# Grouped-query attention in a two-block kernel: value projections placed behind the query projections, their weights' low parts made by GpSimd

## The reference, cut to what matters

```
def attention_module(hx, hc, wq, wk, wv, wo, q_g, k_g, cos, sin, need_ctx):
    qx = apply_rope(rmsnorm((hx @ wq).reshape(B, S, 16, 64), q_g), cos, sin)
    kx = apply_rope(rmsnorm((hx @ wk).reshape(B, S, 4, 64), k_g), cos, sin)
    vx = (hx @ wv).reshape(B, S, 4, 64)
    kc = rmsnorm((hc @ wk).reshape(B, L, 4, 64), k_g)
    vc = (hc @ wv).reshape(B, L, 4, 64)
    k_all = concatenate([kx, kc]); v_all = concatenate([vx, vc])
    # softmax(q k_all / 8) v_all, four query heads on each key head, then @ wo
```

## Time and profile before

| what | value |
|---|---|
| median of 3 runs | 3340.39 us (3338.66 to 3344.8) |
| the profiled execution, first to last instruction | 3345.0 us |
| PE busy | 3225.9 us (96%) |
| DVE busy | 1487.9 us (44%) |
| ACT busy | 1193.4 us (36%) |
| POOL busy | 763.8 us (23%) |
| granted clock of PE, mean | 0.988 of full speed |

### The profile page before, as it was taken

One profiled execution on the slowest core, in us unless ns is written; L12 is line 12 of the kernel. 1 busy time (PEld: TensorE's weight loads), 2 busy tenths in 40 slices (PEclk: granted clock), 3 DMA queues, 4 the chain that ended last, 5 costly groups with the idle time before them and its releaser, 6 DMA issues.

```text
span 3345.0 us, 38977 instructions
## 1 busy us (share of the span) xinstructions
PE 3225.9 (96%) x15760; PEld 2474.1 (74%) x15760; DVE 1487.9 (44%) x2166; ACT 1193.4 (36%) x1764; POOL 763.8 (23%) x399
## 2 busy tenths in 40 slices
PE   6999999999999999999999899999999979999998
PEld 4657777777665777777777576888888658868887
DVE  3572243132357114313269746223333899653234
ACT  3443234233344223423331154211112548632223
POOL 4303334434330343434310000000000039500000
PEclk9999999999999999999999999999999989999999
DMA  6413444544340455465335311222222110123322
GB/s 233 124 43 107 145 126 137 163 141 149 115 133 19 128 160 171 148 191 160 125 91 127 84 48 35 70 63 64 63 63 63 38 38 1 35 67 88 108 87 77
DMA packets 429893, 337.23 MB, mean 101 GB/s; under 512 B 16637, under 2 KB 411223, under 8 KB 417428
## 3 DMA queue, kind: packets, MB, share of 16 engines
q1 hardware_dynamic: 428272, 334.23, 32.9%
q0 software_dynamic: 1248, 0.46, 0.1%
q10 hardware_dynamic: 196, 0.07, 0.0%
HBM read 319.58 MB, written 2.10 MB: 96 GB/s over the span
## 4 chain that ended last, share of the span: by engine, by line
PE 59%; DVE 6%; ACT 2%; POOL 1%; issue 1%; SPq 0%; DMA 0%; DVEq 0%; ACTq 0%
PE PS L423 17%; PE PS L424 17%; PE PS L425 17%; PE PS L771 1%; POOL p L2478 1%; PE PS L586 1%; PE PS L512 1%; DVE both_tmp L1289 1%; PE PS L565 1%; PE PS L1075 1%; PE PS L1076 0%; PE PS L1044 0%; PE PS L1055 0%; DVE stat_r L1272 0%; DVE stat_t L1266 0%
## 5 line engine op out<-in xcount | busy, mean ns | idle before, releaser
L423 PE MATMUL PS<-Hh,Wh 128*128 128x512 f32 x2208 | 877.0, 397 | 13.7 <-DVE Hl L1303 9.4
L424 PE MATMUL PS<-Hl,Wh 128*128 128x512 f32 x2208 | 861.8, 390 | 0.0
L425 PE MATMUL PS<-Hh,Wl 128*128 128x512 f32 x2208 | 861.3, 390 | 0.0
L2433 POOL TENSOR_TENSOR Wl<-raw,Wh 128x1024 fp32r<-128x1024 f32 (+2 forms) x254 | 568.9, 2244 | 1099.3 <-ACT Wh L1950 1099.3
L1950 ACT ACTIVATE Wh<-raw 128x1024 fp32r<-128x1024 f32 (+2 forms) x442 | 436.1, 987 | 404.4 <-PE PS L425 394.2
L423 PEld LDWEIGHTS PS<-Hh,Wh 128*128 128x128 f32 x2208 | 416.0, 188 | 139.1 <-issue 74.0
L425 PEld LDWEIGHTS PS<-Hh,Wl 128*128 128x128 f32 x2208 | 415.6, 188 | 87.8
L424 PEld LDWEIGHTS PS<-Hl,Wh 128*128 128x128 f32 x2208 | 416.2, 188 | 67.2 <-issue 3.5
L1212 DVE TENSOR_TENSOR Wl<-raw,Wh 128x1024 fp32r<-128x1024 f32 (+3 forms) x188 | 217.5, 1157 | 386.2 <-ACT Wh L1950 385.7
L1858 DVE SCALAR_TENSOR_TENSOR cv<-PS,vcols,cv 128x510 f32<-128x510 f32 (+1 forms) x176 | 123.7, 745 | 295.7 <-ACT cv L2357 295.7
L423 PE MATMUL PS<-g_h,Wh 128*128 128x512 f32 x528 | 211.2, 400 | 0.0
(11 more groups left out here) (370 smaller groups left out, 4827.0 us busy)
## 6 DMA issues: line engine op xcount, KB each, us to landing
raw<-in_ffn_w SPq DMA_DIRECT2D x108, 512.0 KB, 3.8
mod_w<-in_w_mod SPq DMA_DIRECT2D x48, 1024.0 KB, 5.6
raw<-in_w_up SPq DMA_DIRECT2D x88, 512.0 KB, 3.8
mod_w<-in_w_ada SPq DMA_DIRECT2D x40, 1024.0 KB, 6.0
raw<-in_w_in SPq DMA_DIRECT2D x62, 512.0 KB, 4.1
UQ<-U SPq DMA_DIRECT2D x128, 99.4 KB, 2.2
raw<-in_w_down SPq DMA_DIRECT2D x32, 384.0 KB, 3.4
raw<-in_conv_w_pw SPq DMA_DIRECT2D x24, 512.0 KB, 4.6
```

The lines of the kernel that those rows point to most:

```text
L423: pe.matmul(o, wh, xh, start=start, stop=False, skip_group_check=True)
L424: pe.matmul(o, wh, xl, start=False, stop=False, skip_group_check=True)
L425: return pe.matmul(o, wl, xh, start=False, stop=stop, skip_group_check=True)
L2433: pool.tensor_tensor(low, src, high.bitcast(F32), ALU.subtract).then_inc(*mark("w_low_pool", one[0]))
```

## The change

In `attention_jobs` the two value slabs go from behind the keys to behind the queries. The norms of the context keys stay at positions 4 and 5, which are query slabs now. The last value slab is turned into token order no longer at the end of the stage but in `gqa_attend` behind the scores of the second tile, in banks 4 and 5. GpSimd makes the low parts of all 12 slabs (`by_pool`), in the order of the list; it splits the context's keys behind the slabs of positions 6 and 7, and the context's values, each half on its own, behind the last slab. The first scores wait for the context's keys only, and the first product with values for all of it. Three small edits are cut below: the context's `hc` buffers no longer have a second place, `vt_c` moves to a free one, and `h_of` follows.

```
@@ -343,8 +343,8 @@
 
     sums_over = {}
 
-    attention_jobs = ([("k2", "x", p) for p in range(KVH // 2)] + [("v2", "x", i) for i in range(2)]
-                      + [("q2", "x", j) for j in range(KD)])
+    attention_jobs = ([("k2", "x", p) for p in range(KVH // 2)] + [("q2", "x", j) for j in range(KD)]
+                      + [("v2", "x", i) for i in range(2)])
     CTX_HEADS = KVH // 2 + 2
 
     def stream(job):
@@ -370,7 +370,7 @@
 
     def by_pool(key):
 
-        return key[0] in BLOCK_1_SLABS or key[0:2] == ("dn", 1)
+        return key[0] in BLOCK_1_SLABS or key[0:2] == ("dn", 1) or key[0] in ("k2", "v2", "q2")
 
     def low_ready(key):
         return ready("w_low_pool" if by_pool(key) else "w_low", key)
@@ -785,13 +785,12 @@
             linear_pair_both(tag, *((("k2", "x", p), wk(p), "split") for p in range(2)))
             jobs = attention_jobs
             head_stat(jobs[0])
-            for i in range(2, len(jobs) + 1):
-                if i < len(jobs):
-                    name, _, g = job = jobs[i]
-                    if name == "v2":
-                        linear_both(job, a["attn_wv_2"][0, :, g * P:(g + 1) * P], c_tag)
-                    else:
-                        linear(job, job, a["attn_wq_2"][0, :, g * P:(g + 1) * P], SEQ)
+            for i in range(2, len(jobs)):
+                name, _, g = job = jobs[i]
+                if name == "v2":
+                    linear_both(job, a["attn_wv_2"][0, :, g * P:(g + 1) * P], c_tag)
+                else:
+                    linear(job, job, a["attn_wq_2"][0, :, g * P:(g + 1) * P], SEQ)
                 one = jobs[i - 1]
                 if one[0] == "v2":
                     values_turned(one, SEQ)
@@ -813,9 +812,12 @@
         def ctx_key_stat(g):
             stat(("ss", "k2", "c", g), [(("k2", "c", g), 0, P, True, True)], CTX, "blocks")
 
-        def values_turned(job, n):
-
-            begin(("turned", *job))
+        def values_turned(job, n, b=None):
+
+            if b is None:
+                begin(("turned", *job))
+            else:
+                begin_at(("turned", *job), b, 1)
             pe.wait_ge(*free(("v2", "x", job[-1]) if job[0] == "v2" else job))
             for t in range(n // P):
                 c = slice(t * P, (t + 1) * P)
@@ -1036,7 +1038,7 @@
                 job, g = ("s2", h, i), h * KVH // G_HEADS
                 begin_at(job, 2 * (n % 2), 2)
                 if (h, i) == (0, 0):
-                    pe.wait_ge(*ready("ctx_parts"))
+                    pe.wait_ge(*ready("ctx_parts", "k_low", 1, 1))
                 if h % 2 == 0 and i == 0:
                     pe.wait_ge(*ready("low_parts", ("q2", "x", h // 2)))
                 q, b = q_parts[:, h, i * P:(i + 1) * P], bank_of[job]
@@ -1069,6 +1071,8 @@
                     begin(job, "mod")
                 pe.wait_ge(*free(("pt2", h, 2 * half + 1)))
                 pe.wait_ge(*free(("pt2_ctx", u)))
+                if u == 0:
+                    pe.wait_ge(*ready("ctx_parts"))
                 o = bank(job)[:, half * 2 * P:(half + 1) * 2 * P]
                 for kb in range(KT):
                     v = v_parts[:, kb, g, h % 2:h % 2 + 2, :].rearrange("p b d -> p (b d)")
@@ -1079,6 +1083,10 @@
             for n in range(len(tiles) + 7):
                 if n < len(tiles):
                     scores(n, *tiles[n])
+                if n == 1:
+                    last = attention_jobs[-1]
+                    values_turned(last, SEQ, 4)
+                    values_turned(("v2", "c", last[-1]), CTX, 5)
                 if n >= 8 and n % 2 == 0:
                     pv((n - 8) // 2)
                 if 0 <= n - 4 < len(tiles):
@@ -2424,13 +2432,18 @@
     def _(pool):
         for i, (o, src) in enumerate(pieces[1]):
             pool.dma_start(o, src).then_inc(*mark("vec_in_rest", *([i] if i + 1 < len(pieces[1]) else []), by=16))
-        for d, one in enumerate(slabs):
-            if not by_pool(one[0]):
-                break
+        def weight_low(d):
+            one = slabs[d]
             src, high = halves(one, raw[d % RAW], Wh[d % WS])
             _, low = halves(one, raw[d % RAW], Wl[d % WS])
             pool.wait_ge(*ready("w_high", one[0]))
             pool.tensor_tensor(low, src, high.bitcast(F32), ALU.subtract).then_inc(*mark("w_low_pool", one[0]))
+
+        number = {one[0]: d for d, one in enumerate(slabs)}
+        for d, one in enumerate(slabs):
+            if not by_pool(one[0]):
+                break
+            weight_low(d)
 
 
         w_dw = vec("w_dw", 0, TAPS * KD).rearrange("p (t j) -> p t j", j=KD)
@@ -2453,10 +2466,7 @@
             inst.then_inc(*mark("ctx_parts", *event))
             return ready("ctx_parts", *event)
 
-        pool.wait_ge(*ready("x_new", ("ffn", 0, "x"), KD - 1))
-        pool.wait_ge(*ready("head_scaled", "k2", "c", KVH // 2 - 1))
-        pool.wait_ge(*free(("turned", "v2", "c", 1)))
-        for e in range(2):
+        def ctx_keys(e):
             at_e = slice(e * HD, (e + 1) * HD)
             src = k_ctx[at_e, 0:KVH // 2, :]
             for d in range(2):
@@ -2465,13 +2475,27 @@
                 low = pool.tensor_tensor(k_lo[d * HD:(d + 1) * HD, e::2, SEQ:], src, k_hi[at_e, e::2, SEQ:].bitcast(F32),
                                          ALU.subtract)
                 pool.wait_ge(*own(low, "k_low", e, d))
-        for c in range(2):
+
+        def ctx_values(c, *event):
             v = v_ctx[:, :, c * P:(c + 1) * P].rearrange("p t (g d) -> p t g d", g=2)
             one = v_parts[:, QT:, 2 * c:2 * c + 2, :, :]
             for b in (0, 2):
                 pool.wait_ge(*own(pool.tensor_copy(one[:, :, :, b, :], v), "v", c, b))
-            i = pool.tensor_tensor(one[:, :, :, 1, :], v, one[:, :, :, 0, :].bitcast(F32), ALU.subtract)
-        own(i)
+            low = pool.tensor_tensor(one[:, :, :, 1, :], v, one[:, :, :, 0, :].bitcast(F32), ALU.subtract)
+            pool.wait_ge(*own(low, *event))
+
+        for i, job in enumerate(attention_jobs):
+            weight_low(number[job])
+            e = i - CTX_HEADS - KVH // 2
+            if 0 <= e < 2:
+                pool.wait_ge(*low_ready(job))
+                pool.wait_ge(*ready("x_new", ("ffn", 0, "x"), KD - 1))
+                pool.wait_ge(*ready("head_scaled", "k2", "c", KVH // 2 - 1))
+                ctx_keys(e)
+        pool.wait_ge(*low_ready(job))
+        for c, event in enumerate((("v_low", 0), ())):
+            pool.wait_ge(*free(("turned", "v2", "c", c)))
+            ctx_values(c, *event)
         for n in range(G_HEADS * QT):
             h, i = divmod(n, QT)
             pool.wait_ge(*ready("sum_inverse", n))
```

More of the change, by code:

```diff
@@ L215, in write @@
     STATS = {"x": (SV, SY, ST, SR), "c": tuple(at(f"ctx_stat{i}", 52 + i, [CTX]) for i in range(4))}
-    HC = {c0: [at(f"hc_{x}{c0}", kb, [KD, CTX], F32R) for x, kb in (("h", c0), ("l", c0 + 8))] for c0 in (0, 56)}
+    HC = [at(f"hc_{x}", kb, [KD, CTX], F32R) for x, kb in (("h", 56), ("l", 64))]
     FIRST = MOD_COLS
@@ L265, in write @@
     YB = at("YB", 24, [KD, BOTH])
-    vt_c = [at(f"vt_c{i}", 16 + i, [CTX]) for i in range(2)]
+    vt_c = [nc.alloc_sbuf_tensor_at(f"vt_c{i}", [P, CTX], F32, offset=int(kc_base + 4 * MOD_COLS + i * KB)) for i in range(2)]
     KT = (SEQ + CTX) // P
@@ L360, in h_of @@
             return Hh, Hl
-        return HC[0 if tag[0:2] == ("n", 1) else 56]
+        return HC
     def head_in(job):
```

## The result

The changed kernel takes 3346.07 us, median of 18 runs (3343.92 to 3355.59); the kernel before, run beside it, 3339.28 us, median of 18 (3337.19 to 3355.79). The ratio is 1.0018, with a 95% interval from 1.0012 to 1.0024: 6.0 us slower (4.0 to 8.0), inside the 0.2% (6.7 us) that were named as no change, though the interval reaches beyond it. Forecast was +3.7, at 3344.1 us.

A forecast was written before the change was run, and what follows sets the result against it. DVE was taken to bound the way to GpSimd's first scaling. The terms -11.5 + 15.8 - 5.3 + 1.2 - 0.4 + 1.3 + 2.6 gave +3.7 us on 3340.4, so 3344.1 us, range 3335 to 3352.

The forecast's parts named there:

- DVE's ledger: DVE's time from its last context activation to the first tile's minimum: 108.0 us, 10.2 of them waits, taken as decisive.
- Ten low parts leave, nine hold: In the ledger: ten low parts leave DVE, -11.5 us; nine on GpSimd hold it 1.75 each, +15.8 us.
- rival B: In the stage: holds cost little, as lows meet waits and PSUM instructions; 15.8 goes, 3328.3 us; chance 0.09.
- rival D: In the stage: every low costs its full 2.08 us, 3.0 more, 3347.1 us; chance 0.12.
- the holds they cost DVE stay: Context keys' instructions on GpSimd move into two pieces between weights; their holds on DVE were to stay unchanged.
- The norm: Ahead of the ledger: GpSimd's early low part holds DVE some 2.1 us, of which PE notices +1.3 us.
- DVE's waits that vanish: In the stage: with values behind queries, DVE gets its next work earlier, -5.3 us.
- the end of the stage: Ahead of the first minimum: DVE waits for the last values, turned behind two tiles' scores, +1.2 us.
- PE's stalls at `ctx_key_stat`: At the context keys' statistics: PE waits about 7 and 3 us for bank 6, the clock falls, +2.6 us.
- Order and GpSimd apart: Whole change split in halves: the new order alone worth some -2 us, GpSimd's part +5.6 us.
- Rival A: Between fourth and sixth query: GpSimd's queue runs late, PE waits 3.9 us for a low; 3348.7 us; chance 0.17.
- Rival C: In the stage: PE leads and the values fill its hole, -12.3 us, 3328.1 us; chance 0.04.

The follow-up runs named there:

- act_v: Changed kernel's order with DVE's low parts, context-key statistics in bank 7, last values turned right behind their product, ScalarE reading the heads' statistics: 3324.60 us.
- twice_tt: Changed kernel, but GpSimd writes each low part of the query and value slabs twice by the same two-input subtraction: 3362.41 us.
- bank7: Changed kernel with the context keys' statistics in bank 7 in place of bank 6: 3339.96 us.
- pool_only: Kernel before with its own order of work, but GpSimd makes the ten low parts: 3344.82 us.
- order_only: Changed kernel with its new order, but DVE makes the ten low parts as before: 3335.63 us.

## Why the prediction was right, point by point

**DVE's ledger sets the stage: right.** act_v took 7.4 us of DVE work out and the stage followed by 5.4; twice_tt put 15.1 in and it followed by 15.3. PE's wait of 8.1 us in bank7 cost DVE hardly anything, since DVE was behind.

**Ten low parts leave, nine hold: right in both terms.** Forecast 15.8 us for the nine, measured 15.7, with single ones from 1.08 to 2.08. None fell into a wait as a whole (rival B; the one of 2634.95 did in part and cost the least, 1.08), and only some cost the full 2.08 (rival D). With the 11.5 taken off this leaves +4.2. Against it stands a term that I had put at "the holds they cost DVE stay": the splits of the context's keys and values held DVE 2.7 us instead of 4.5, 1.8 less. The traces show where. The values' part fell from 1.1 to 0.1 us, since they are split at the end of the stage now, mostly beside DVE's waits and its instructions on PSUM. The keys' part fell from 3.3 to 2.6: their first low parts (2687.03, 2.60 us) lie mostly in DVE's wait of 2.44 us that ends at 2688.91. In bank7, without that wait, the keys hold DVE 4.8 us.

The Trainium skill (SBUF — State Buffer, section "SBUF: two separate sides") describes an exclusive lock on a port pair that GpSimd shares with DVE's instructions of two SBUF inputs. The subtractions agree with it: of the 2.61 us of the one at 2647.95 DVE's L1577 lost 2.06, and it had begun 0.40 later. The one-input instruction agrees less: it costs 0.72 us once, and another such DVE instruction runs beside it at its usual 0.69.

**The norm: right.** Forecast +1.3, measured 29.53 - 28.21 = 1.3, the same in pool_only and bank7, 0.0 to 0.2 in the kernels without GpSimd's low parts, and 3.5 in twice_tt, which holds there twice.

**The waits: right in place, too small in size.** This is the step that was off. I took -5.3 for DVE's waits that vanish, +1.2 for the end of the stage and +2.6 for PE's stalls at `ctx_key_stat`, -1.5 in all; the ledger shows 13.3 - 10.2 = +3.1. The first rotation's wait of 3.75 was foreseen. The end of the stage has 1.54 and 1.31 us of waits for the turned values where 1.2 was taken. The two query products behind PE's stalls bring waits of 4.26 and 2.44, 6.7 together, against 1.3 + 2.6 = 3.9. The stalls themselves were forecast well (7 and 3 against 7.69 and 2.71), but I wrote that "DVE's backlog covers that wait, not what the clock does with it". It doesn't cover it. The first product behind a stall takes 8.2 us (2666.84 to 2675.05), the second 6.7 (2680.29 to 2686.99), against 5.9: a slow clock can be 2.3 + 0.8 = 3.1 of the 6.7 (3.5 by the 5.7 us that order_only shows for the second at full clock). The rest is the stall itself. bank7 takes the stalls away and the slow clock behind the first with them, and 5.9 of the 6.7 go. DVE's own low parts would have filled 2.3 us of these waits, as they do in order_only; so much of the 11.5 us taken off DVE brought nothing.

**Order and GpSimd apart: sign and size right, their sum not.** Forecast -2 and +5.6; measured -4.0 (-7.0 to -1.0) and +6.3 (+3.3 to +9.4). The prediction added two halves that interact, by some 3 us of stage: the stalls cost 5.8 us with GpSimd's low parts and 2.7 without. It is not that the holds lengthen the stalls much (7.69 and 2.71 us with them, 7.06 and 2.71 without), but that DVE has less of its own to do while PE is late.

**The end.** Of the 0.4 us between scalings that were to go, 0.24 is left. The first scaling came 0.39 us earlier than before on the two traces' own scales, where 2751 had been named; but the work ahead of the norm came 7.85 earlier, so it is 7.5 us late: 5.5 in the stage and 2.0 ahead of it, of which PE, by the norm, notices 1.3. From there to the end of the execution the changed one takes 597.9 us and the one before 597.1, so that "ends a constant time after" holds to 0.7 us.

**Rival A** was right in its mechanism and wrong in its price: PE waits 3.7 us for GpSimd's low part, over the 3 us that were named as its sign, and DVE waits for nothing behind it. **Rival C** did not happen: PE waits for L1271 four times, 13.5 us in all, and DVE has more to do, not less.

**Luck.** The waits were 4.6 us larger than forecast and the context's holds 1.8 smaller, so part of the miss was made up by a term that had been put at nothing. The 7.5 us of the traces, one execution each, lie at the upper end of the interval of the times, 4.0 to 8.0. That the forecast of 3.7 comes near 6.0 is partly chance.

What stays open: how the 6.7 us share out between stall and clock more finely than above. No run holds the clock fixed.

## What to carry to other kernels

Work moved to an idle engine isn't free if its instructions hold those of the busy one: here a subtraction of 1.15 us on DVE became one of 2.4 us on GpSimd that cost DVE 1.74. Look for an engine whose instructions do not hold the busy one (in act_v's stage DVE's instructions were lengthened beside GpSimd's alone): twelve reads of a PSUM bank moved to ScalarE gained about what ten low parts on GpSimd lost (5.4 to 6.9 us of stage against 5.3 to 8.1).

When the order of work changes, follow each bank (or buffer) to who frees it, with the bounding engine's own lateness added. Work taken off an engine just ahead of its wait only lengthens the wait: 2.3 us of the 11.5 went so here. Run the halves of a change apart before their sum is believed.

A wait of an engine that runs ahead is worth nothing until it is longer than its lead. PE waited 8.1 us for a low part at a price of 0.8 us or less, and 7.7 us for a bank, with a slow clock behind it, at a price of some 4.

## What the runs showed of the hardware, unexpected

- On GpSimd a one-input TENSOR_SCALAR of 128x1024 holds one DVE instruction of two SBUF inputs for under 0.8 us, or none, and the next ones beside it not at all; the two-input subtraction of the same size held for 1.1 to 2.1 us, nine times in the changed kernel. In the tiles, L1930 (two SBUF inputs) ran seven times beside a scaling of p and took 0.68 us each time.
- Holding goes both ways: GpSimd's low part takes 2.42 us where DVE was idle as it began (2634.95), and up to 2.99 where a DVE instruction was under way (2605.09). The one-input scaling of p takes 2.52 to 2.55 us instead of 2.21 the six times that it began beside L1930.
- The granted clock fell to its lower level, 1.2 GHz, in PE's waits or just behind them, and came back while PE worked. In the changed kernel PE does nothing from 2658.5 to 2666.2, and the clock is 0.50 from 2662.0 to 2672.2. In bank7, with no wait over 2.9 us there, it is 1.00 from 2655.0 to 2670.1; from 2683.7 to 2690.5 it is 0.50, where PE stands for GpSimd until 2686.5.
